# Mixture-of-experts results: added per token in DRAM in every round, instead of gathered and combined behind the rounds

## The reference

```python
combine = jnp.sum(jax.nn.one_hot(expert_id, N_EXPERTS, dtype=f32) * (g_w * top_w)[..., None], axis=1)
out = jnp.zeros_like(x)
for e in range(N_EXPERTS):
    hid = jax.nn.silu(x @ lp['exp_gate'][e]) * (x @ lp['exp_up'][e])
    out = out + combine[:, e:e + 1].astype(x.dtype) * (hid @ lp['exp_down'][e])
...
x = x + g2[:, None, :] * hier_moe(modulate(x, lp['norm2_g'], sh2, sc2), lp)
```

## Time and profile before

| | |
|---|---|
| runs, median (lowest to highest) | 1013.62 us (1003.34 to 1017.67), 3 runs |
| the profiled execution | 1007.72 us, its span 1005.8 us |
| mean granted TensorE clock in it | 0.926 |
| TensorE busy | 858.0 us (85%) |
| DVE, ACT, POOL busy | 421.4, 259.1, 81.0 us |
| DMA | 236.91 MB, mean 236 GB/s |

### The profile page before, as it was taken

One profiled execution on the slowest core, in us unless ns is written; L12 is line 12 of the kernel. 1 busy time (PEld: TensorE's weight loads), 2 busy tenths in 40 slices (PEclk: granted clock), 3 DMA queues, 4 the chain that ended last, 5 costly groups with the idle time before them and its releaser, 6 DMA issues. The chain is left out here.

```text
span 1005.8 us, 18868 instructions
## 1 busy us (share of the span) xinstructions
PE 858.0 (85%) x8174; PEld 503.1 (50%) x8174; DVE 421.4 (42%) x795; ACT 259.1 (26%) x502; POOL 81.0 (8%) x133
## 2 busy tenths in 40 slices
PE   3799999997987777599999799932999999999950
PEld 1365555453655556589998555531344433334320
DVE  1221573323328887758786466450222010010007
ACT  2231222222357765132322311110111111111102
POOL 1420000001000000212221000030000000000012
PEclk9999999999969997799999699955999999999995
DMA  9920624362899991203332452099999999999817
GB/s 322 338 53 21 230 84 168 109 224 94 349 406 406 405 401 63 55 14 71 86 93 66 127 200 84 1 338 387 388 391 351 385 398 389 408 382 432 346 69 287
DMA packets 60130, 236.91 MB, mean 236 GB/s; under 512 B 7428, under 2 KB 12452, under 8 KB 53648
## 3 DMA queue, kind: packets, MB, share of 16 engines
q1 hardware_dynamic: 47472, 205.78, 54.4%
q0 software_dynamic: 5632, 13.97, 4.6%
q10 hardware_dynamic: 6944, 15.95, 4.5%
HBM read 167.10 MB, written 65.96 MB: 232 GB/s over the span
## 5 line engine op out<-in xcount | busy, mean ns | idle before, releaser
L2235 PE MATMUL ps<-arena 128*32 128x512 f32 (+2 forms) x800 | 168.8, 602 | 1.7 <-ACT arena L2313 1.7
L721 PE MATMUL ps<-arena 128*128 128x512 f32 (+3 forms) x448 | 123.6, 435 | 0.0
L2235 PEld LDWEIGHTS ps<-arena 128*32 128x32 f32 (+2 forms) x800 | 60.3, 136 | 101.5 <-issue 98.5
L721 PEld LDWEIGHTS ps<-arena 128*128 128x128 f32 (+1 forms) x448 | 68.1, 189 | 59.9 <-issue 59.0
L2255 PE MATMUL ps<-arena 128*32 128x512 f32 (+2 forms) x400 | 84.8, 594 | 1.5 <-ACT arena L2317 1.5
L1913 PE MATMUL ps<-arena 128*128 128x512 f32 x160 | 73.4, 614 | 1.9 <-PEq L1334 1.9
L588 DVE SCALAR_TENSOR_TENSOR arena<-arena 128x128 f32<-128x128 f32 (+3 forms) x56 | 30.9, 552 | 82.6 <-ACT arena L457 81.1
L654 PE MATMUL ps<-arena 128*128 128x512 f32 (+1 forms) x160 | 54.2, 498 | 1.1 <-ACT arena L415 1.1
L2440 DVE TENSOR_TENSOR arena<-arena,ps 128x512 f32<-128x512 f32 x12 | 8.3, 688 | 111.6 <-ACT arena L2309 111.6
L2255 PEld LDWEIGHTS ps<-arena 128*32 128x32 f32 (+2 forms) x400 | 30.1, 135 | 48.0 <-issue 47.3
L1913 PEld LDWEIGHTS ps<-arena 128*128 128x128 f32 x160 | 30.7, 197 | 37.4 <-issue 37.4
(11 more groups left out here) (339 smaller groups left out, 1311.7 us busy)
## 6 DMA issues: line engine op xcount, KB each, us to landing
gathered_tokens<-arena SPq DMA_DIRECT2D x16, 2560.0 KB, 26.8
arena<-in_exp_gate_dram SPq DMA_DIRECT2D x16, 2048.0 KB, 14.2
arena<-in_exp_up_dram SPq DMA_DIRECT2D x16, 2048.0 KB, 16.9
arena<-in_exp_down_dram SPq DMA_DIRECT2D x16, 2048.0 KB, 15.2
arena<-in_w_mod_dram SPq DMA_DIRECT2D x12, 2048.0 KB, 12.7
arena<-in_w_in_dram SPq DMA_DIRECT2D x4, 2048.0 KB, 8.6
expert_outputs<-arena SPq DMA_DIRECT2D x1, 6144.0 KB, 30.7
expert_outputs<-arena ACTq DMA_DIRECT2D x12, 512.0 KB, 10.3
```

The lines of the kernel that those rows point to most:

```text
L721: mm = pe.matmul(ps[0:m, b, 0:hi - lo], ring[:, slot_of(what), k, (e % 4) * P:(e % 4) * P + m], hT[:, k, lo:hi], start=(k == 0), stop=(k = ...
L2235: mm = pe.matmul(ps[c:c + m, b, :], xgT[:, k, c:c + m], w[n % 3][:, k, :], start=(k == 0), stop=(k == KT - 1))
```

## The change

Three things change.

A token's result is no longer put together at the end. A DRAM tensor `token_sums` gets the residual rows `xs2` from SP in the routing block. In each round DVE multiplies the 128 result rows, on their way out of PSUM, by "gate rows" (`gw`: weight of the row times `g2`), and POOL adds them to `token_sums` with an indirect DMA that accumulates. Where a round holds two experts a token may stand in both, so there are two such DMAs, the second after the first has landed: the first takes the rows of the first expert, the second all 128, with those of the first expert sent to rows that nobody reads (`ASIDE`).

For this a row of a round must know its token and its weight. A DRAM tensor `row_shares` has three numbers for each row of each expert's part: the token, the weight if it is a context token, the weight if it is a latent one. It is filled early with rows that point to unused sums; at the start of the expert block POOL scatters the shares of all tokens into it (ten indirect DMAs of 128 rows of 12 bytes). In each round ACT loads the 128 shares (`load_tokens`), and DVE turns them into indices and gate rows (`tokens`).

The block at the end is left with three copies from `token_sums` to the outputs. `expert_outputs`, its fill, its stores, `result_rows` and the tables for it are gone.

The diff, without the changes of the path for experts with too many rows, of the constants, and of lines that only rename:

```diff
+        sums_d = nc.dram_tensor("token_sums", (ASIDE + P, D), F32, kind="Internal").ap()
+        share_d = nc.dram_tensor("row_shares", (NE * TR, 3), F32, kind="Internal").ap()
...
+                for tt in range(NTT - 1):
+                    sp.wait_ge(x2_ok, tt + 1)
+                    sp.dma_start(sums_d[tt * P:(tt + 1) * P, :], xs2[:, tt, :]).then_inc(sums_ok, 16)
...
+                sp.wait_ge(x2_ok, NTT)
+                sp.dma_start(sums_d[(NTT - 1) * P:T, :], xs2[:, NTT - 1, :]).then_inc(sums_ok, 16)
...
-                        pe.wait_ge(yo_a, r)
-                        pe.wait_ge(yo_v, r)
+                        pe.wait_ge(yo_ok, 2 * r)
...
-                    mm.then_inc(y6_mm, 1)
+                        mm.then_inc(y6_mm, 1)
...
-                def y_out(r):
-                    act.wait_ge(y6_mm, r + 1)
+                def load_tokens(r):
                     if r:
-                        act.wait_ge(y_st, 16 * r)
-                    act.activation(yo[:, 0:512], ps[:, Y0, :], ACT.Copy).then_inc(yo_a, 1)
-                    act.wait_ge(yo_a, r + 1)
-                    act.wait_ge(yo_v, r + 1)
-                    act.dma_start(yg_d[r * P:(r + 1) * P, :], yo).then_inc(y_st, 16)
+                        act.wait_ge(yo_ok, 2 * r)
+                    for n, c0, q0, nq in SEGS[r]:
+                        row = row_at(act, n) if n else 0
+                        src = share_d[bass.ds(row + QROWS * q0, QROWS * nq), :] if n else share_d[QROWS * q0:QROWS * (q0 + nq), :]
+                        act.dma_start(got[QROWS * c0:QROWS * (c0 + nq)], src).then_inc(ld_tok, 16)
...
+                act.wait_ge(shared, 32 * NTT)
+                load_tokens(0)
                 for r in range(1, NR):
                     sigmoid(r)
                     if r + 1 < NR:
                         x_out(r + 1)
                     if r + 3 < NR:
                         load_rows(act, r + 3)
-                    y_out(r - 1)
                     h_out(r)
-                y_out(NR - 1)
-                act.wait_ge(y_st, 16 * NR)
+                    load_tokens(r)
...
+                def shares():
+                    ch(dve.memset(share, 0.0))
+                    ch(dve.tensor_copy(share[:, :, :, 0], cst("token").unsqueeze(1).to_broadcast([P, 2, NTT])))
+                    ch(dve.tensor_copy(share[:, :, 0, 1], wsel[:, :, 0]))
+                    dve.tensor_copy(share[:, :, 1:, 2], wsel[:, :, 1:]).then_inc(share_ok, 1)
+
+                def gate_rows():
+                    ch(dve.tensor_scalar(gw, gate2[:, 0, :], got[:, 1:2], None, ALU.mult))
+                    ch(dve.scalar_tensor_tensor(gw, gate2[:, 1, :], got[:, 2:3], gw, ALU.mult, ALU.add))
+
+                def tokens(r):
+                    dve.wait_ge(ld_tok, 16 * sum(len(SEGS[i]) for i in range(r + 1)))
+                    if r > 1:
+                        dve.wait_ge(added, tok_adds(r - 1))
+                    b, at = SEGS[r][0][3], 2 * (r % 2)
+                    ch(dve.tensor_copy(add_f[:, 0:1], got[:, 0:1]))
+                    if b < 4:
+                        ch(dve.tensor_scalar(add_f[:, 1:2], got[:, 0:1], cst("of_last")[:, b:b + 1], cst("of_first")[:, b:b + 1], ALU.mult, ALU.add))
+                        dve.tensor_copy(add_i[:, at:at + 2], add_f).then_inc(tok_ok, 1)
+                    else:
+                        dve.tensor_copy(add_i[:, at:at + 1], add_f[:, 0:1]).then_inc(tok_ok, 1)
+                    gate_rows()
...
                 def y_out(r):
-                    dve.wait_ge(y6_mm, r + 1)
-                    if r:
-                        dve.wait_ge(y_st, 16 * r)
-                    dve.tensor_copy(yo[:, 512:], ps[:, Y0 + 1, :]).then_inc(yo_v, 1)
-
+                    for half in range(2):
+                        cols = slice(512 * half, 512 * half + 512)
+                        dve.wait_ge(y6_mm, 2 * r + half + 1)
+                        if r:
+                            dve.wait_ge(added, tok_adds(r))
+                        dve.tensor_tensor(yo[:, cols], ps[:, Y0 + half, :], gw[:, cols], ALU.mult).then_inc(yo_ok, 1)
+
+                weigh(3, NTT)
+                shares()
+                dve.wait_ge(sums_ok, 16 * NTT)
                 hidden(0)
                 hot = overflow_table()
                 for r in range(1, NR):
+                    tokens(r - 1)
                     hidden(r)
+                    y_out(r - 1)
                     if r == 1:
                         overflow_rows(hot)
-                    if r == 2:
-                        result_rows()
-                        weigh(3, NTT)
-                    y_out(r - 1)
+                tokens(NR - 1)
                 y_out(NR - 1)
...
+                def add_rows(index, n):
+                    return pool.indirect_dma_start(out=sums_d, out_offset=bass.IndirectOffsetOnAxis(ap=add_i[0:n, index:index + 1], axis=0),
+                                                   in_=yo[0:n, :], in_offset=None, compute_op=ALU.add)
+
+                pool.wait_ge(share_ok, 1)
                 for tt in range(NTT):
-                    for r, dst in enumerate((yA, yB)):
+                    for r in range(2):
                         pool.indirect_dma_start(
-                            out=dst[:, tt, :], out_offset=None, in_=yg_d,
-                            in_offset=bass.IndirectOffsetOnAxis(ap=back_i[:, r * NTT + tt:r * NTT + tt + 1], axis=0)).then_inc(got[tt], 16)
-
-            @block.vector
-            def _(dve):
-                ch = Chain(dve, dve7)
-                for tt in range(NTT):
-                    cc = 0 if tt == 0 else 1
-                    dve.wait_ge(got[tt], 32)
-                    dve.wait_ge(first7, tt + 1)
-                    ch(dve.scalar_tensor_tensor(yA[:, tt, :], yB[:, tt, :], wsel[:, 1, tt:tt + 1], yA[:, tt, :], ALU.mult, ALU.add))
-                    ch(dve.tensor_tensor(yA[:, tt, :], yA[:, tt, :], gate2[:, cc, :], ALU.mult))
-                    dve.tensor_tensor(yA[:, tt, :], yA[:, tt, :], xs2[:, tt, :], ALU.add).then_inc(y7, 1)
+                            out=share_d, out_offset=bass.IndirectOffsetOnAxis(ap=slot_i[:, r * NTT + tt:r * NTT + tt + 1], axis=0),
+                            in_=share[:, r, tt, :], in_offset=None).then_inc(shared, 16)
+                pool.wait_ge(sums_ok, 16 * NTT)
+                for r in range(NR):
+                    pool.wait_ge(tok_ok, r + 1)
+                    pool.wait_ge(yo_ok, 2 * r + 2)
+                    if r:
+                        pool.wait_ge(added, tok_adds(r))
+                    b, at = SEGS[r][0][3], 2 * (r % 2)
+                    add_rows(at, QROWS * b).then_inc(added, 16)
+                    if b < 4:
+                        pool.wait_ge(added, tok_adds(r) + 16)
+                        add_rows(at + 1, P).then_inc(added, 16)
...
+        st7 = sem("st7")
+
+        with nc.Block() as block:
+            @block.sync
+            def _(sp):
+                sp.dma_start(y_prompt[0], sums_d[0:P, :]).then_inc(st7, 16)
+                sp.dma_start(y_sample[0, 0:2 * P, :], sums_d[P:3 * P, :]).then_inc(st7, 16)
+                sp.wait_ge(st7, 48)
 
             @block.scalar
             def _(act):
-                for tt in range(NTT):
-                    act.wait_ge(got[tt], 32)
-                    act.activation(yA[:, tt, :], yA[:, tt, :], ACT.Copy, scale=wsel[:, 0, tt:tt + 1]).then_inc(first7, 1)
-
-            @block.sync
-            def _(sp):
-                for tt in range(NTT):
-                    sp.wait_ge(y7, tt + 1)
-                    dst = y_prompt[0] if tt == 0 else y_sample[0, (tt - 1) * P:tt * P, :]
-                    sp.dma_start(dst, yA[:, tt, :]).then_inc(st7, 16)
-                sp.wait_ge(st7, 16 * NTT)
+                act.dma_start(y_sample[0, 2 * P:, :], sums_d[3 * P:T, :]).then_inc(st7, 16)
 
 
 # ---- launch: one core; inputs and outputs as the reference has them ----
```

More of the change, by code:

```diff
@@ L117, in const_table @@
     put("cap_rows", np.broadcast_to(cap[place], (P, NE)))
-    put("out_row", np.broadcast_to((np.cumsum(cap) - cap)[place], (P, NE)))
+    put("token", np.arange(P)[:, None] + P * np.arange(NTT))
+    first = np.arange(P)[:, None] < QROWS * np.arange(4)
+    put("of_last", ~first)
+    put("of_first", first * (ASIDE + np.arange(P)[:, None]))
+    pads = out[0:PAD_PARTS, NCONST:].reshape(PAD_PARTS * PAD_ROWS, 3)
+    pads[:, 0] = T + np.arange(TR)
+    out[0:PAD_PARTS, NCONST:] = pads.reshape(PAD_PARTS, 3 * PAD_ROWS)
     return out
@@ L1785, in build @@
         cnt, ntile, incl, one16, spare = (small_view(NE) for _ in range(5))
-        key, rank, over, capE, outE, ovsum, ovpos = (small_view(NE) for _ in range(7))
+        key, rank, over, capE, ovsum, ovpos = (small_view(NE) for _ in range(6))
         sq, sq2 = small_view(NE, NE), small_view(NE, NE)
         plan_f, over_f = small_view(2, NE), small_view(1 + 2 * NOV)
-        back_f, limit_f = small_view(2, NTT), small_view(2, NTT)
```

(20 more changed lines are left out.)

95 lines of the change are left out of this document (42 added, 53 removed).

## The result

| | before | after |
|---|---|---|
| runs, median (lowest to highest) | 1012.22 us (1003.34 to 1018.95, and one of 1213.2), 20 runs | 1018.49 us (1012.41 to 1024.49), 20 runs |
| ratio to before, with 95% interval | | 1.0078 [1.0057, 1.0099] |
| the profiled execution, its span | 1007.72, span 1005.8 | 1015.07, span 1013.3 |
| first transposed row to the end of the last down product ("the rounds") | 696.65 to 971.15: 274.5 | 696.68 to 984.86: 288.2 |
| from there to the close ("the tail") | 34.7 | 28.4 |

The changed kernel is slower by 0.8%; the medians lie 6.3 us apart. The ratio compares fast runs alone, so before's run of 1213.2 us is not in it. The measured 1018.49 lies above the forecast's own range (992 to 1013), though inside the one for all cases (990 to 1040), and the time moved the other way.

What follows compares the result with a forecast made beforehand. TensorE's own work was taken to bound the rounds, with DMA queues also full. Span 1005.8 - 10.5 (tail) + 1 (start) + 3 (rounds) = 999.3, plus 1.9 around it 1001.2, forecast 1004; own range 992 to 1013, all cases 990 to 1040.

Steps and rivals of the forecast that it cites:

- the 3 us put on the rounds: Expert rounds: loss expected from the chain of scatters, mainly before the last down product; 3 us, 0 at the least.
- the 23.8 us of a pair: Rounds with two experts: two chained scatters take 19.8 us, or 23.8 with 2 us more each for the second read.
- 24.2 us a pair: Rounds 5, 6 and 7, pairs in a row: together they allow 72.5 us, 24.2 a pair, before TensorE waits.
- rival 1: Expert rounds: the chain of scatters sets the round; 1036 us at 15 us a scatter, 1072 at 18; chance 0.25.
- rival 2: Rounds 3 to 8, full queues: extra DMA bytes make 2.7 to 13 us of backlog, delaying weights; 1006 to 1019; chance 0.10.
- 11.2 us of slack: Round 11's last up weights: they land at 936.8 and are used from about 948, so 11.2 us of delay is free.
- Nothing is lost: Rounds, before the hidden product: DVE's added work and the share load fit ahead of it, costing TensorE 0 us.
- the 5.4 us of slack: Rounds: the hidden product ends near 17 us and is due at 22.4, leaving 5.4 us.
- The start: Before the rounds: SP's extra store of the fifth residual tile delays the row scatters; 1 us taken, 1.4 at most.
- Rival 3: Start of the expert block: the share scatter lands late and TensorE waits about 10 us once; 1014; chance 0.08.
- the last sentence of the prediction: TensorE's gaps: if the clock fell below 1.00 in them, each would cost more than its length; no size given.
- The tail: Last down product to close: 24 us instead of 34.6, a gain of 10.5; 14.5 with lower ends, 1.7 with upper.

Runs made afterwards that it cites:

- e3: The changed kernel with the same 19 scatters made plain, overwriting rows instead of adding to them; 1001.37 us, ratio to before 0.9871.
- e1: The changed kernel with DVE's hidden product put ahead of the index operations and gate rows; ratio to before 1.0047.
- e2: The changed kernel with two buffers for the shares, each share load issued a round earlier; ratio to before 1.0047.
- e5: On e2, a second result buffer, so a result waits for the adds of the round before the last; ratio to before 1.0009.
- e4: The changed kernel without the adds of rounds 0 to 10, those of round 11 kept; 1004.68 us, ratio to before 0.9910.
- e7: On e5, the second scatter of a pair takes only the second expert's rows, not all 128; ratio to before 0.9962.
- e9: On e7, the hidden product of round 1 stands ahead of the index operations of round 0; 1007.97 us, ratio to before 0.9937.
- e10: The changed kernel with one edit: the second scatter of a pair takes only the second expert's rows; ratio to before 1.0016.

## Why the prediction was wrong

**The cause, in one sentence.** An adding row holds its DMA engine 337 ns where a plain one takes 165; that made a pair of scatters 26.7 us instead of the 23.7 of e3, where 24.2 were allowed, and ate the slack of the weights, for which TensorE waits in e1, e2 and e5.

**The step that failed: the 3 us put on the rounds, and in it the 23.8 us of a pair.** The mechanism was right and the term too small. The prediction allowed 24.2 us a pair and took 23.8: "At my value the chain just fits; every us beyond costs 3 there." A pair measured 26.7 and the rounds lost 13.7: a pair is 2.1 from the landing of the pair before to its first add, where 0.7 was taken; 0.3 between the two; and two scatters, six of which take 12.2 on average (12.8, 14.9, 9.2, 15.8, 7.6, 12.6), where 8.5 + 10.3 with 2 each gives 11.4. That is 1.4 from the result (both of its halves stand behind the wait for the adds, and the sum counted one) and 1.5 from the scatters. The price of the adding itself was nearly right: e3's six average 10.7, so it is 1.5 a scatter for the 2 taken. What was low is the plain scatter beside the weights, 10.7 for 9.4. By the prediction's own rule 2.5 us over costs 7.6, and 7.5 were measured; with e3's 23.7 it gives 0, and so it was. (In e1, e2 and e5 the hidden product or the share load stands elsewhere, so the rule doesn't apply to them.) This is rival 1's mechanism at a lower price than rival 1 gave it. The rest of the 13.7 are 1.9 more of waits elsewhere, mostly round 1's, 2.6 of clock, 0.7 of the first gate product, and 1 us in small parts.

**DMA bytes, rival 2.** Its clause "unless an adding packet holds its engine longer than its bytes; at twice that, 15 us" is nearest to what happened: 2.04 times, 18.2 us of backlog. The Trainium skill ("Collectives: The Full Stack", "The bandwidth ceiling: the fold count and why AG ≠ RS ≠ AR") says of the reduce step of a ring of cores that its two source reads halve the rate. The 2.04 of this case, measured on an indirect DMA, agrees with it. The sum had the adding only as 2 us on a scatter's landing; rival 2 put the backlog by bytes at 2.7 to 13 us and, behind 11.2 us of slack, at about 2. The adding acts on everything else in the queues too: the weights land in 22 to 23 us for 14 to 17, and share loads in 10.8 us (885.76 to 896.60), for the 10 taken.

**"Nothing is lost" before the hidden product** was wrong in round 1. Shares issued at 719.64, on time, landed at 738.45 beside the first experts' weights; e4 has the same wait of 2.4 us with no adds before it, so this one has nothing to do with the adding. Elsewhere the 5.4 us of slack held until the results came late.

**The start**: 1 us was put on it; the two executions show none, though others of this stage come up to 9 us later, so 1 us can't be told. **Rival 3**, the share scatter, didn't occur: ACT issued the first share load at once behind its copy. **The clock** fell behind the gaps, as the last sentence of the prediction warned, and cost 2.6 us that no term had.

**The tail**: 6.3 us won for 10.5. Of the 28.4 us, 3.0 lie between the last down product and the end of the result (0.7 taken): the last share load is issued when the result before is written, and that waits for adds. The two scatters and the gaps to them took 11.8 (11.3 taken), the change of block 2.9 (1.7), the copies 10.3 (10), and the close 0.4. e2 to e7 and e9, whose shares come earlier or whose chain is shorter, have 24.5 to 26.5; the forecast had 24.1.

**The sum**: 1001.2 for the profiled execution, against 1015.07. The tail missed 4.2, the rounds 10.7 (3 taken, 13.7 measured), the start -1. e3, without the adding, takes 1003.23 us in its profiled execution and 1001.37 in the median: near the forecast, but the forecast had 4 us a pair for the adding in it, so part of this is luck. Two small slips of the range have no bearing on the result: the tail's lower ends give a gain of 13.9, not 14.5, and the 992 leaves out the 1 us of the start and the 2.9 that the forecast adds for the median.

**Not settled**: why e3's plain scatters take 10.7 us beside the weights where 9.4 were taken from the earlier trace rows, and how the 13.7 us would be shared between chain and queue if only one were there. e5 loosens the chain and still waits 5.8 for weights, and e10 shortens both at once.

## What to carry to other kernels

Price an accumulating DMA by its engine time, here twice a plain one's, and charge it to every other transfer of the stretch: where the queues are full, the weights and the small loads pay. Then send no row through it that isn't needed: the scatter of all 128 rows with some aimed at dummy rows cost more than an extra load of indices. When a chain has less than 1 us to spare, count both ends of each link (here the result's two halves), for with three pairs in a row its overrun comes back three times over; and when one wait is removed, read the next two waits before expecting its length back.

## What the hardware showed that was not expected

- Adding to DRAM with quiet queues, issue to landing: 4.6 us for 64 rows and 6.2 for 128, where the plain scatters of e3 take 3.2 and 4.2. The rows, of the changed kernel's tail and of e3's:

```profile
token_sums<-arena,add_i POOLq DMA_INDIRECT x1, 4.6
token_sums<-arena,add_i POOLq DMA_INDIRECT x1, 6.2
```

```profile
token_sums<-arena,add_i POOLq DMA_INDIRECT x1, 3.2
token_sums<-arena,add_i POOLq DMA_INDIRECT x1, 4.2
```

- POOL is busy longer with an adding scatter too: 1.55 us for 128 rows, and 0.95 for a plain one (0.98 for a gather in the earlier trace rows).
- A load of 12 bytes to each of 128 partitions, 1.5 KB in all, takes 10 to 19 us beside weight loads, at least as long as a store of 512 KB (10.3 in the earlier trace rows). The 19 are from 719.64 to 738.45 us in the changed kernel.
- DRAM to DRAM, 2560 KB in three transfers took 10.3 us from the first issue to the last landing.
